# RWKV operands and triangular inverses in one program, row turns behind the pair products, and the samples' new states built in the layout of the output

## The chip, the cores and the metric

One core of a Trainium2 chip runs the whole step. The metric is the device time of one execution in microseconds. Of the kernel before, three timed runs gave a median of 1883.43 us (1877.42, 1883.43, 1886.05).

## The reference, cut to what matters

Two decoder layers are run for 256 prompt tokens and for 8 samples of 8 tokens each (320 token columns). The change lies in the RWKV-7 head group of the first layer (8 heads of 64):

```python
def rwkv7_scan(r, w, k, v, a, b, S0):
    def step(S, inp):                       # S is [value, key], per head
        rt, wt, kt, vt, at, bt = inp
        sa = jnp.einsum('bhvk,bhk->bhv', S, at)
        S = S * wt[:, :, None, :] + sa[..., None] * bt[:, :, None, :] + vt[..., None] * kt[:, :, None, :]
        return S, jnp.einsum('bhvk,bhk->bhv', S, rt)
    S, y = lax.scan(step, S0, xs)
    return y, S
```

Its final S is an output: `new_rwkv_prompt` (one state, 8 heads of 64 x 64) and `new_rwkv_sample` (8 states of that size). Before and after it stand the projections and the latent attention (MLA); behind it the output projection, a dense SwiGLU, the GLA layer and a mixture of 8 experts.

## The kernel before, in words

The step is a chain of parts. Between two parts stands `next_part()` (L154 to L159): all engines meet at a barrier, the semaphores are cleared, and they meet again. Inside a part every engine has its own list of instructions, written out by hand in the order in which it runs, and the engines wait for one another on semaphores. A `with nc.Block()` is such a set of lists; its end also holds every engine until all are there. So nothing of a later block starts before the last engine of the earlier one is through. No weights are loaded in the RWKV part: its only transfers are its own inputs and its outputs, issued on SP's queue.

The RWKV part has three blocks. Tokens are in three tiles (`TILES`: two of 128 prompt tokens, one of the 64 sample tokens), and "turning" means a transpose on TensorE.

1. The operands block (L1188 to L1394). VectorE and ScalarE build the scaled vectors b (`bF`), k (`kF`), and the pair `AR` of a and r, all with features on the partitions. TensorE turns v into rows by token (L1356) and the samples' old states into `S0T` (L1382). Last it turns b and k into rows, `rowB` and `rowK`, six turns of up to four 128 x 128 blocks (L1393) in banks 0 to 3; VectorE (L1280) and ScalarE (L1325) take them out of the banks by turns. `bonus` (L1275) is finished before them.
2. The inverses block (L1396 to L1487). The products b·a and b·r of each tile (`pairs`, L1419, 64 x 64 weights, 128 columns) are masked into `BM` (L1456), and `XT` and `X` are begun from it (L1466 to L1468). Then come five levels (L1427) in which TensorE and VectorE take turns; k's pair products and their masked form `KM` are woven into the first three.
3. The states block (L1490 to the next `next_part`). Chunk by chunk the prompt's state advances (`step`, L1560; `advance`, L1671 and L1673), the part of the output that comes from the state is added (`from_state`, L1567; `y_add`, L1677), and U of the samples gives their output (L1635, L1636). ScalarE begins the layer norm's terms after the third `from_state` (L1761, L1762). The samples' new states are made head by head: VectorE spreads U and v over eight blocks of columns, one for a sample (`spread`, L1683 and L1684, two buffers), TensorE multiplies (L1577, L1578, 64 x 64 weights and 512 columns), VectorE adds the old state and multiplies by the decay (`new_state`, L1689, L1690). Only when all four pairs of heads are done does TensorE turn the prompt's and the eight samples' states into the outputs' layout (L1654), ScalarE and VectorE copy them out by turns (L1767, L1741), and SP stores them one by one, 128 KB each (L241).

## Time and profile before

| | |
|---|---|
| median of three runs | 1883.43 us |
| profiled execution, its own time | 1890.77 us |
| its span, first to last instruction | 1888.9 us |
| mean granted TensorE clock | 0.962 |
| TensorE busy / weight loads / VectorE / ScalarE | 1790.3 / 1148.9 / 666.3 / 353.5 us |
| MLA part's last work to the part behind RWKV's first | 330.79 to 492.80 us |

How to read it: a time such as 376.84 is in us from the start of the span, "x80" is the number of records (a float32 matmul leaves two, a turn one), and "[0.93 <-PEq L1189]" says how long the engine had been idle before the line and what ended that. In the tables by stretch, PEclk is the granted clock: 1.00 is 2.4 GHz, 0.50 is 1.2 GHz. "PEld" is the weight load.

### The profile page before, as it was taken

How to read it: one execution, taken by the hardware profiler on the slowest of the kernel's cores; microseconds unless marked ns; L12 is line 12 of the kernel's file. 1: busy time of each engine (PE TensorE's matmuls, PEld its weight loads, DVE VectorE, ACT ScalarE, POOL GpSimd, SP SyncE). 2: the span in 40 equal slices, each digit the busy share in tenths (PEclk: the TensorE clock that was granted, in tenths of full speed). 3: DMA queues.
4: the chain of work that ended last, by engine and by line, in shares of the span. 5: the costliest groups of instructions: out<-in, count | busy, mean ns of one | idle time of the engine just before them, and what ended most of it. 6: DMA issues, size and time to landing. Idle time of an engine off the chain costs nothing.

```text
span 1888.9 us, 42360 instructions
## 1 busy us (share of the span) xinstructions
PE 1790.3 (95%) x19238; PEld 1148.9 (61%) x19238; DVE 666.3 (35%) x1243; ACT 353.5 (19%) x584; POOL 29.7 (2%) x37
## 2 busy tenths in 40 slices
PE   7989898689799999998999999999999999999997
PEld 6957564587599999996833535344353443535344
DVE  4534332774675554656642110121102111120121
ACT  3223231501243332444310000000000000000002
POOL 0010000000000000000000000000000000000000
PEclk9989998698799999999989999999999999999998
DMA  9130540200654444425499999999999999997994
GB/s 289 45 109 1 150 142 11 37 3 2 181 155 142 150 145 126 155 68 150 143 379 416 417 412 417 397 382 417 364 417 373 405 409 366 417 354 290 399 416 159
DMA packets 166440, 463.28 MB, mean 245 GB/s; under 512 B 27770, under 2 KB 110876, under 8 KB 135412
## 3 DMA queue, kind: packets, MB, share of 16 engines
q1 hardware_dynamic: 164910, 457.37, 65.2%
q8 instruction: 151, 2.47, 0.5%
q0 software_dynamic: 1152, 3.15, 0.4%
q14 instruction: 29, 0.24, 0.0%
q10 hardware_dynamic: 198, 0.05, 0.0%
HBM read 451.57 MB, written 8.95 MB: 244 GB/s over the span
## 4 chain that ended last, share of the span: by engine, by line
PE 52%; DVE 1%; ACT 0%; issue 0%; DVEq 0%; ACTq 0%
PE bank L2623 46%; PE bank L2591 1%; PE bank L310 1%; PE bank L312 1%; PE bank L311 1%; PE bank L2554 0%; PE bank L2475 0%; PE bank L2597 0%; PE bank L2561 0%; PE bank L2490 0%; PE bank L2509 0%; PE bank L2482 0%; ACT ring L2787 0%; DVE mixT L2805 0%; PE bank L2494 0%; PE bank L2686 0%
## 5 line engine op out<-in xcount | busy, mean ns | idle before, releaser
L2623 PE MATMUL bank<-ring,x 128*32 128x512 f32 (+1 forms) x6144 | 587.5, 540 | 0.0
L2623 PEld LDWEIGHTS bank<-ring,x 128*32 128x32 f32 x6144 | 195.0, 110 | 359.9 <-issue 357.2
L2623 PE MATMUL bank<-ring,hid 128*32 128x256 f32 x5376 | 291.5, 379 | 0.0
L2623 PEld LDWEIGHTS bank<-ring,hid 128*32 128x32 f32 x5376 | 174.7, 110 | 117.1 <-issue 3.1
L310 PE MATMUL bank<-x_hi,w_hi 128*128 128x320 f32 (+1 forms) x488 | 151.8, 311 | 0.0
L312 PE MATMUL bank<-x_hi,w_lo 128*128 128x320 f32 (+1 forms) x488 | 150.8, 309 | 0.0
L311 PE MATMUL bank<-x_lo,w_hi 128*128 128x320 f32 (+1 forms) x488 | 150.8, 309 | 0.0
L2129 DVE TENSOR_TENSOR w_lo<-ring,w_hi 128x2048 fp32r<-128x2048 f32 (+2 forms) x51 | 112.5, 2208 | 96.2 <-ACT w_hi L2053 95.9
L2987 DVE TENSOR_TENSOR hrow<-sil,bank 128x512 f32<-128x512 f32 (+1 forms) x48 | 26.9, 616 | 296.1 <-PE bank L2623 296.1
L2950 DVE TENSOR_TENSOR xT<-xT,bank 128x320 f32<-128x320 f32 x56 | 23.5, 483 | 277.4 <-PE bank L2591 277.4
L2053 ACT ACTIVATE w_hi<-ring 128x2048 fp32r<-128x2048 f32 (+2 forms) x51 | 94.1, 1846 | 128.9 <-PE bank L312 124.3
L2769 ACT ACTIVATE sil<-bank 128x512 f32<-128x512 f32 (+1 forms) x48 | 22.6, 544 | 478.9 <-PE bank L2623 478.9
L310 PEld LDWEIGHTS bank<-x_hi,w_hi 128*128 128x128 f32 (+1 forms) x488 | 90.9, 186 | 1.9 <-issue 1.0
L311 PEld LDWEIGHTS bank<-x_lo,w_hi 128*128 128x128 f32 (+1 forms) x488 | 90.9, 186 | 0.6 <-issue 0.2
L312 PEld LDWEIGHTS bank<-x_hi,w_lo 128*128 128x128 f32 (+1 forms) x488 | 90.9, 186 | 0.4
L2776 ACT ACTIVATE Y<-bank 128x256 f32<-128x256 f32 x24 | 7.5, 384 | 403.8 <-PE bank L2623 403.8
L310 PE MATMUL bank<-hid,w_hi 128*128 128x320 f32 x240 | 75.2, 313 | 4.1 <-DVE w_lo L2129 4.1
L311 PE MATMUL bank<-hid,w_hi 128*128 128x320 f32 x240 | 74.8, 312 | 0.0
L312 PE MATMUL bank<-hid,w_lo 128*128 128x320 f32 x240 | 74.8, 312 | 0.0
L2969 DVE COPY listed<-bank 32x2 f32<-32x2 f32 x108 | 16.5, 153 | 145.9 <-PE bank L2597 144.5
L310 PE MATMUL bank<-proj_x_hi,proj_w_hi 128*128 128x320 f32 (+1 forms) x160 | 51.2, 320 | 6.5 <-DVE proj_w_lo L587 6.5
L311 PE MATMUL bank<-proj_x_lo,proj_w_hi 128*128 128x320 f32 (+1 forms) x160 | 50.5, 316 | 0.0
(569 smaller groups left out, 2209.7 us busy)
## 6 DMA issues: line engine op xcount, KB each, us to landing
ring<-in_moe_w_gu SPq DMA_DIRECT2D x128, 1024.0 KB, 15.9
ring<-in_moe_w_down SPq DMA_DIRECT2D x112, 1024.0 KB, 13.1
ring<-in_moe_w_gu SPq DMA_DIRECT2D x128, 768.0 KB, 10.7
ring<-in_ffn_w_gu_even SPq DMA_DIRECT2D x44, 512.0 KB, 4.9
pages<-in_cache_mla SPq DMA_DIRECT2D x128, 144.0 KB, 2.4
ring<-in_w_in_odd SPq DMA_DIRECT2D x12, 1024.0 KB, 5.6
ring<-in_ffn_w_down_even SPq DMA_DIRECT2D x10, 1024.0 KB, 5.1
proj_ring<-in_w_in_even SPq DMA_DIRECT2D x9, 1024.0 KB, 8.0
```

The source lines that it names most:

```text
L310: t.matmul(out, w_hi, x_hi, start=start, stop=False)
L311: t.matmul(out, w_hi, x_lo, start=False, stop=False)
L312: return t.matmul(out, w_lo, x_hi, start=False, stop=stop)
L2053: s.activation(whi[:, i % NSP, 0:size(i)], ring[:, i % NS, 0:size(i)], ACT.Copy).then_inc(hi_ready, 1)
L2129: v.tensor_tensor(wlo[:, i % NSP, 0:size(i)], ring[:, i % NS, 0:size(i)], whi[:, i % NSP, 0:size(i)].bitcast(F32), ALU.subtract).then_inc( ...
L2591: mm = t.matmul(ps[banks[y]][:, 0:TOK], Y[part, s_, z * P:(z + 1) * P], selT[part, s_, :], start=(s_ == 0), stop=(s_ == SG - 1), tile_posi ...
L2623: mm = t.matmul(ps[banks[g3]][SL * y:SL * y + SL, 0:w], act[:, g3, k, :], m_ring[:, slot, at + y * w:at + (y + 1) * w], start=start, stop= ...
L2769: ins = s.activation(sil[:, s_, 0:quarter(g)], ps[s_][:, 0:quarter(g)], ACT.Silu)
L2776: s.activation(Y[:, s_, :], ps[bank][:, 0:256], ACT.Copy).then_inc(y_ready, 1)
L2950: last = v.tensor_tensor(xT[:, 2 * y + z, :], xT[:, 2 * y + z, :], ps[bank][:, 0:TOK], ALU.add)
L2969: last = v.tensor_copy(listed[SL * y:SL * y + SL, s_, :], ps[6][SL * s_:SL * s_ + SL, 0:2])
L2987: ins = v.tensor_tensor(hrow[:, 512 * s_:512 * s_ + n], sil[:, s_, 0:n], ps[3 + s_][:, 0:n], ALU.mult)
```

## The change

- The operands and inverses blocks become one block, with no meeting of the engines in between. The order of TensorE's list changes: the b pair products of the three tiles come first, as soon as `AR`, `bonus` and the `S0T` copies are done; the rows of b and k are turned behind them, in banks 6 and 7, and all go out of the banks on ScalarE. VectorE copies no rows.
- VectorE multiplies the samples' b and k by their decay at the end (`bks`, eight instructions of 128 x 64) ahead of `bonus`. The fifth turn puts the decayed b rows of the samples into partitions 0 to 63 and the k rows into 64 to 127 of `rowB[:, 2]`. Likewise the samples' v rows are made a second time in partitions 64 to 127 of `rowK[:, 2]` (four more matmuls and one ScalarE copy of 64 x 512), and U is later written into partitions 0 to 63 of it.
- VectorE begins tiles 0 and 1 of the inverse, takes the first level of tile 0, then begins tile 2.
- In the states block the rows of b and k, not those of U and v, are spread over the samples (`BKb`, 128 partitions, eight instructions in place of sixteen, four at the block's start and four between `rhs2` and the first state). `S0T` is multiplied by the decay there too, in place. TensorE then makes each new state already turned: for every sample and head one product of `S0T` with the identity and one of `UV2` (U over v, 128 partitions) with `BKb`, both with 64 weight columns and 64 columns moved, added in the bank: 128 products, in banks 0, 1, 4 and 6. There are no adds and decays behind them and no turns of the samples.
- Four copies take them out (VectorE pairs 0 and 2, ScalarE 1 and 3), and SP stores four times 256 KB, each for all samples and one pair of heads, then the prompt's state. `y_add(2)` now waits for the third `from_state`, as `y_add(3)` does.

The diff, cut to its core:

```diff
-                            for n in range(0, 6, 2):
-                                v.wait_ge(row_full, n + 1)
-                                r = TILES[n % 3][1]
-                                v.tensor_copy((rowB, rowK)[n // 3][0:r, n % 3, :], ps[n % 4][0:r, :]).then_inc(row_dve, 1)
+                            v.wait_ge(k_ready, 4)
+                            for n, src in enumerate((bF, kF)):
+                                for c in range(4):
+                                    last = v.tensor_tensor(bks[:, n, c, :].rearrange("p (b t) -> p b t", t=DS), src[:, c, SEQ:TOK].rearrange("p (b t) -> p b t", t=DS),
+                                                           wends[:, c, :].rearrange("p (b o) -> p b o", o=1).to_broadcast([P, NB, DS]), ALU.mult)
+                            last.then_inc(bks_ready, 1)
...
+                            v.wait_ge(st_full, NB)
+                            v.wait_ge(stored.sem, stored.n)
+                            begin(0)
+                            begin(1)
+                            for li in range(5):
+                                tiles = [i for i in range(3) if li < len(LEVELS[i])]
+                                for i in tiles:
+                                    r = TILES[i][1]
+                                    if li == 0 and i == 1:
+                                        begin(2)
...
-                            for n in range(1, 6, 2):
+                            for n in range(5):
                                 s.wait_ge(row_full, n + 1)
-                                r = TILES[n % 3][1]
-                                s.activation((rowB, rowK)[n // 3][0:r, n % 3, :], ps[n % 4][0:r, :], ACT.Copy).then_inc(row_act, 1)
+                                s.activation(ROWS[n], ps[6 + n % 2][:, :], ACT.Copy).then_inc(row_act, 1)
...
+                                    if i == 2:
+                                        t.matmul(ps[7][64:128, cols], vT[:, c, lo:lo + r], C("ident"), start=True, stop=True, tile_position=(0, 64))
...
+                            t.wait_ge(ar_ready, 1)
+                            t.wait_ge(bonus_ready, 1)
+                            t.wait_ge(st_free, NB)
                             for i in range(3):
-                                pairs(i, bF, (2 * i, 2 * i + 1)).then_inc(b_full, 1)
+                                pairs(i, bF, (2 * i, 2 * i + 1)).then_inc(pairs_full, 1)
+                            for n in range(5):
+                                t.wait_ge(*((k_ready, 4) if n < 4 else (bks_ready, 1)))
+                                if n >= 2:
+                                    t.wait_ge(row_act, n - 1)
+                                for c in range(4):
+                                    cols = slice(c * P, (c + 1) * P)
+                                    if n < 4:
+                                        src, lo = (bF, kF)[n // 2], TILES[n % 2][0]
+                                        mm = t.transpose(ps[6 + n % 2][:, cols], src[:, c, lo:lo + P], C("ident"))
+                                    else:
+                                        for q in range(2):
+                                            mm = t.matmul(ps[6][64 * q:64 * q + 64, cols], bks[:, q, c, :], C("ident"), start=True, stop=True, tile_position=(0, 64 * q))
+                                mm.then_inc(row_full, 1)
...
+                            def new_states(pr):
+                                for b in range(NB):
+                                    for h in (2 * pr, 2 * pr + 1):
+                                        hs, _, _ = head(h)
+                                        t.matmul(ps[N_BANK[pr]][hs, b * RD:(b + 1) * RD], S0T[:, b, pr, :], C("ident")[:, hs], start=True, stop=False, tile_position=(0, hs.start))
+                                        mm = t.matmul(ps[N_BANK[pr]][hs, b * RD:(b + 1) * RD], UV2[:, h * RD:(h + 1) * RD], BKb[:, h, b, :], start=False, stop=True,
+                                                      tile_position=(0, hs.start))
+                                mm.then_inc(n_full, 1)
...
-                            new_states((0, 1))
+                            t.wait_ge(blk_ready, 1)
+                            t.wait_ge(s0_ready, 1)
+                            new_states(0)
                             step(3)
+                            new_states(1)
                             from_state(3)
-                            new_states(range(2, RH))
+                            new_states(2)
+                            new_states(3)
...
+                            for pr in range(4):
+                                last = v.tensor_tensor(S0T[:, :, pr, :], S0T[:, :, pr, :], wends[:, pr, :].rearrange("p (b o) -> p b o", o=1).to_broadcast([P, NB, RD]), ALU.mult)
+                            last.then_inc(s0_ready, 1)
+                            for h in range(4, RH):
+                                last = spread(h)
+                            last.then_inc(blk_ready, 1)
...
+                            for pr in (1, 3):
+                                s.wait_ge(n_full, pr + 1)
+                                s.activation(news[:, pr, :, :].rearrange("p b k -> p (b k)"), ps[N_BANK[pr]][:, :], ACT.Copy).then_inc(n_act, 1)
+                            s.wait_ge(o_full, 1)
+                            s.activation(srow2, ps[5][0:RD, :], ACT.Copy).then_inc(o_act, 1)
...
+                            for pr in range(4):
+                                sp.wait_ge(n_act if pr % 2 else n_dve, pr // 2 + 1)
+                                store(sp, O["new_rwkv_sample"][0, :, 2 * pr:2 * pr + 2].rearrange("b h v k -> (h v) b k"), news[:, pr, :, :])
+                            sp.wait_ge(o_act, 1)
+                            store(sp, O["new_rwkv_prompt"][0, 0].rearrange("h v k -> v h k"), srow2.rearrange("v (h k) -> v h k", h=RH))
+                            sp.wait_ge(stored.sem, stored.n)
```

## Rows read from the trace of the kernel before

**Rows 1.** The page: span, then the chain of waits by engine.
```profile
span 1888.9 us, 42360 instructions
PE 52%; DVE 1%; ACT 0%; issue 0%; DVEq 0%; ACTq 0%
```
**Rows 2.** Timeline, end of the part: start us, us, engine, line, operation, [idle before].
```profile
480.73 5.92 PE L1654 MATMUL bank<-consts,S0T 128*64 128x128 f32 x32
...
481.59 0.64 SPq L241 DMA_DIRECT2D out_new_rwkv_prompt<-rwT  x1
482.54 6.08 SPq L241 DMA_DIRECT2D out_new_rwkv_sample<-rwT  x8
492.80 5.34 SPq L1895 DMA_DIRECT2D ring<-in_w_out_even  x4
```
**Rows 3.** Windows of one us: PE, PEld, DVE, ACT, POOL, PEclk, DMA share, GB/s.
```profile
482.00:483.00 1.00, 1.00 (x7) 0.84 (x5) 0.51 (x1) 0.32 (x1) 0.00 (x0) 0.50 0.08 13
...
484.00:485.00 1.00, 1.00 (x7) 0.82 (x6) 0.22 (x1) 0.59 (x1) 0.00 (x0) 0.50 1.02 157
...
490.00:491.00 1.00, 0.00 (x0) 0.00 (x0) 0.00 (x0) 0.00 (x0) 0.00 (x0) 0.50 0.65 95
```
**Rows 4.** Timeline, from the operands into the inverses.
```profile
337.33 0.28 DVE L1211 TENSOR_TENSOR shT<-shT,vecs 128x112 f32<-128x112 f32 x1
...
372.48 1.68 DVE L1275 TENSOR_TENSOR bonus<-bank,rwT 128x320 f32<-128x320 f32 x4
...
376.84 4.13 PE L1419 MATMUL bank<-hT,bF 64*64 64x128 f32 x80 [0.93 <-PEq L1189]
378.89 1.29 DVE L1456 TENSOR_TENSOR BM<-bank,consts 128x512 f32<-128x512 f32 x2 [2.68 <-PE bank L1419]
...
389.14 1.86 PE L1427 MATMUL bank<-X,BM 64*64 64x64 f32 x15 [1.80 <-DVE X L1468]
```
**Rows 5.** Timeline, TensorE and VectorE behind the v rows.
```profile
360.56 2.30 PE L1368 MATMUL bank<-consts,dif 128*128 128x128 f32 x12
362.80 1.68 DVE L1257 TENSOR_TENSOR t<-t,bank 128x320 f32<-128x320 f32 x4
```
**Rows 6.** Timeline of the states block, VectorE and ScalarE, then two of TensorE.
```profile
444.88 0.67 DVE L1703 TENSOR_TENSOR rhs<-rhs,bank 64x512 f32<-64x512 f32 x1
449.03 0.42 DVE L1705 TENSOR_TENSOR ST<-bank,wend 128x256 f32<-128x256 f32 x1 [3.48 <-PE bank L1553]
458.36 0.67 DVE L1683 TENSOR_TENSOR ub<-U,consts 64x512 f32<-64x512 f32 x1
458.96 0.68 DVE L1684 TENSOR_TENSOR vb<-rowV,consts 64x512 f32<-64x512 f32 x1
463.18 1.92 ACT L1761 ACTIVATE hT<-bonus,vecs 128x320 f32<-128x320 f32 x4 [6.09 <-PE bank L1567]
465.00 1.25 ACT L1762 ACTIVATE hT<-gT 128x1280 f32<-128x1280 f32 x1
...
L1623 PE MATMUL bank<-rhs,XT x16: 218/218/218, 450.5 to 451.4; 64*64 64x64 f32 x16
...
458.36 0.66 PE L1567 MATMUL bank<-hT,ST 64*64 64x64 f32 x16
```
**Rows 7.** Count, ns min/median/max, first and last start; last a line of the timeline.
```profile
L1636 PE MATMUL bank<-KM,rowV x16: 218/218/218, 457.1 to 457.9; 64*64 64x64 f32 x16
L1066 PE MATMUL bank<-mixT,uv x32: 222/222/270, 329.2 to 330.1; 128*64 128x64 f32 x32
396.61 1.09 PE L1427 MATMUL bank<-T,XT 64*64 64x64 f32 x16
```
**Rows 8.** Timeline, a weight load behind a change of the array's form.
```profile
442.26 1.72 PEld L1606 LDWEIGHTS bank<-AV,XT 64*64 64x64 f32 x32 [0.20 <-issue]
```
**Rows 9.** Windows: granted clock of two stretches (columns as in rows 3).
```profile
434.00:436.00 2.00, 2.00 (x28) 2.00 (x29) 0.00 (x0) 0.00 (x0) 0.00 (x0) 0.50 0.00 0
456.00:458.00 2.00, 2.00 (x77) 2.00 (x75) 1.07 (x3) 0.66 (x2) 0.00 (x0) 1.00 0.00 0
```

More of the change, by code:

```diff
@@ L1189, in model, with heads @@
+                    LEVELS = [[2, 4, 8, 16, 32], [2, 4, 8, 16, 32], [2, 4]]
+                    BLOCKS = [2, 2, 1]
+                    def heads(bank, r=P):
+                        return ps[bank][0:r, :].rearrange("p (h t) -> p h t", h=RH)
+                    ROWS = [rowB[:, 0, :], rowB[:, 1, :], rowK[:, 0, :], rowK[:, 1, :], rowB[:, 2, :]]
                     with nc.Block() as block:
@@ L1276, in _, with masked @@
                             last.then_inc(bonus_ready, 1)
[L1277 to L1280 removed]
                             v.wait_ge(bonus_ready, 1)
+                            def masked(dst, i, banks, ready):
+                                r = TILES[i][1]
+                                m = C("rw_T" if i < 2 else "sm_T", r).rearrange("p (o a t) -> p o a t", o=1, a=2).to_broadcast([r, 4, 2, RC])
+                                for par in range(2):
+                                    last = v.tensor_tensor(dst[0:r, i, :, :, :].rearrange("p (c e) a t -> p c e a t", e=2)[:, :, par, :, :],
+                                                           ps[banks[par]][0:r, :].rearrange("p (c a t) -> p c a t", c=4, a=2), m, ALU.mult)
+                                last.then_inc(ready, 1)
@@ L1490, in model @@
+                inv.close()
                 with ExitStack() as st:
@@ L1568, in from_state @@
                                 mm.then_inc(y_full, 1)
-                            def new_states(hs_):
-                                for h in hs_:
-                                    h0, pr = 64 * (h % 2), h // 2
-                                    t.wait_ge(blk_ready, h + 1)
-                                    if h % 2 == 0 and pr >= 2:
-                                        t.wait_ge(n_ready, pr - 1)
-                                    out = ps[pr % 2][h0:h0 + 64, :]
-                                    t.matmul(out, rowB[0:64, 2, h * RD:(h + 1) * RD], ub[:, h % 2, :, :].rearrange("p b v -> p (b v)"), start=True, stop=False)
-                                    mm = t.matmul(out, rowK[0:64, 2, h * RD:(h + 1) * RD], vb[:, h % 2, :, :].rearrange("p b v -> p (b v)"), start=False, stop=True)
-                                    mm.then_inc(n_full, 1)
+                            def new_states(pr):
[6 more added lines that the diff above has]
+                                mm.then_inc(n_full, 1)
                             for i in range(2):
```

205 lines of the change are left out of this document (72 added, 133 removed).

## The prediction
> **What bounds the kernel now.** I read four views in this order. First the page: the chain that ended last lies on TensorE in the last layer [rows 1], far behind the change. It says nothing of the RWKV part, for `next_part()` puts a barrier in front of and behind it, so a microsecond taken out there comes out of the total, if nothing behind depends on absolute time, and nothing does: the next weights are asked for only at 492.80, after the barrier [rows 2]. So the part has to be read by itself, from its timeline. In it the last thing is a tail: the reader sees 32 sample turns from 480.73 to 486.65 (plus four of the prompt ahead of them) and nine stores issued from 481.59 to 488.62 [rows 2]. The windows show when those stores end: the DMA engines are idle until nearly 483, then full at some 157 GB/s, and at 490.65 they stop (0.65 of the last us) [rows 3]. The first instruction behind the barrier comes 2.15 us later. So the part ends on its output bytes: 9 x 131 KB = 1.18 MB, at 150 to 157 GB/s 7.6 to 7.9 us, begun only when the last turn chain begins. The timeline of the border between the first two blocks shows a smaller thing: `bonus` is ready at 374.16, yet the first pair product starts at 376.84 [rows 4], because row turns, their copies and the block's end stand between.
>
> **Part by part.**
>
> *Samples' v rows a second time.* Four more float32 products of 128 moved columns, about 0.21 us each, so 0.85 us on TensorE, and one ScalarE copy. What stands behind them is the chain to the spread norms (360.56 to 362.86), taken by VectorE from 362.80 on without idle time before it [rows 5]. The first of the four norm banks needs three of the twelve turns, so it is full near 361.4, 1.4 us before VectorE comes. Shifted by 0.85 it is 0.5 us early, and the later ones come 0.58 us apart against 0.42 us per use, which is about level at the fourth. I take 0; without that cover it costs 0.9.
>
> *`bks`.* Eight VectorE instructions of 128 x 64. The nearest rows: 128 x 112 takes 0.28 us [rows 4]; 512 columns take 0.68 at a pace of 0.60 [rows 6]. That is 0.8 ns a column, so 64 columns last 0.24 and pace 0.17: 8 x 0.17 = 1.36. Bounds: 8 x 0.08 = 0.6 (no fixed cost) and 8 x 0.28 = 2.2. It delays `bonus`, on which the pairs now wait: 374.16 + 1.36 = 375.5.
>
> *One block for two.* Pairs start at 375.5 instead of 376.84: gain 1.3. VectorE masks 2.05 us later, as now (376.84 to 378.89) [rows 4]. The row turns leave VectorE (three copies) and come behind the 4.13 us of pairs, 379.6 on. They are paced by ScalarE, two banks, near 0.65 us each, so they end near 383. In that time VectorE runs begin(0) and begin(1) (3.4 us each, to 384.4), so TensorE's first level of tile 0 is late (383 instead of 381) but nobody is held: VectorE needs it at 384.4. Then comes one `T` (0.6) in front of begin(2), so that the level of tile 2, which opens the rest of the list, starts at 388.35 instead of 389.14 [rows 4]: of the 1.3 us 0.8 is left. Bounds: 0 (if `bks` is at its upper end) and 2 (below).
>
> *States block, front.* The first four spreads run at its start, where VectorE waits about 2 us for its first bank; the copy behind them is 0.4 late, needed only at 438.6. The other eight (four decays of `S0T`, four spreads, 128 x 512, pace 0.60) start when `rhs2` is done, 445.55, and last 4.9 us, to 450.4. The idle gap there is 3.48 us, up to 449.03 [rows 6]. So 1.4 us of them push the first state, and with it the emptying of bank 1 on which the own terms of chunks 2 and 3 wait. That wait was satisfied before TensorE came (U's product ends at 451.5 [rows 6]); now it ends near 451.9. I take +0.5 on TensorE's list, with 0 and 1.4 as bounds.
>
> *States block, products.* In place of 16 products of 512 columns there are 128 of 64 columns, in pairs on one half of the array, then the other. The output product of the samples has just this order: two added products on one half of the columns, then the other half; its 32 records (L1635 and L1636) start from 457.0 to 457.9, so 16 products in 0.95 us, 59 ns each. With 128 rows of weights as here, L1066 has 16 products in 0.95 too, 59 ns. Where all sit on the same tile, eight products of the level (396.61, 16 records) take 0.94 us, 117 ns each [rows 7]. I take 59: the order is that of the first row, and the shape is that of the second. A `new_states(pr)` is 32 x 0.059 = 1.9 us.
>
> A rule of the Trainium skill speaks against this part. First the row: where the weights' form goes from 128*64 to 64*64, the next load comes after 0.20 us of idle time [rows 8]. "TensorEngine Tiling (Array Packing)", Key Properties, says that changing the tiling mode, and not just the tile, drains TensorE. By that rule each swap between `new_states` (128*64) and `step` or `from_state` (64*64) costs, and there are five.
>
> Five such swaps at the 0.20 us of the row are 1.0 us; without them the part would end 0.7 earlier than below (the stores don't wait for all five).
>
> *The tail, put together.* `from_state(2)` ends its issue near 458.9 [rows 6]; the second advance no longer stands behind four spreads, so TensorE is not held there. With +0.5 and a little for `step(2)`: 459.6. Then new(0) to 461.65, step(3) 462.3, new(1) 464.35, `from_state(3)` 465.1, new(2) 467.1, new(3) 469.0, prompt's turns 469.5. ScalarE may start the norm's terms only behind `from_state(3)`, 465.2, and works 3.1 us on them (1.92 + 1.25) [rows 6]. So its first new-state copy is done at 468.9. SP's list is in order, so stores 1 to 4 leave from 469.0 on, and only store 0 (VectorE's, near 464.5) has landed by then. Issue to first bytes is 1.35 us (481.59 to some 482.9) [rows 2, 3]. Left are 3 x 262 + 131 KB = 0.92 MB, at 150 GB/s 6.1 us: 476.4. Plus 2.15 to the next part: 478.6. Now that is 492.8, so the tail gives 14.2.
>
> That assumes the rate of the present 256-byte pieces also for stores over 128 partitions. The pieces stay the same size, so I keep it; bounds 4 us (if more partitions feed it better) and 9 us (if SP or the engines need half as long again for 1024 pieces a store).
>
> *Sum.* 0.8 + 14.2 = 15.0 us. Own time of the profiled execution 1890.8 - 15.0 = 1875.8 (span 1888.9 to 1873.9). That execution is 7.3 above the median of the runs, which I carry along as an offset: 1883.4 - 15.0 = 1868.4.
>
> **The rivals.**
>
> *A. The products don't pair up.* Two products on the same tile in a row may each wait for the other's columns: 117 ns [rows 7]. For it: the 128-row row (L1066) changes halves after each product, this order only after two. Against it: L1635/L1636 change after two and reach 59. Price: a `new_states` is 3.75 us; the norm's terms start 3.7 later and new(3) ends at 476.5; the stores overlap better, store 3 leaves at 477.1, lands at 1.35 + 2.6 later = 481.1, next part 483.2. Gain 9.6 + 0.8 = 10.4: 1873.
>
> *B. Unpaired and at 1.2 GHz.* The granted clock fell to 0.50 in the samples' state products although TensorE was busy all the time; there 28 records stand in 2 us [rows 9]. At 0.50 a level on one tile took 1.86 us to the end of its 15th record (389.14), less 0.3 us for the last one's own length 0.21 for each product [rows 4]. 128 of them take 27 us, 19.6 more than forecast: new(3) ends near 488.6, store 3 leaves at 489.2, next part 495.3. Slower than before by 2.5 - 0.8 = 1.7, some 1885. It decides from about 0.19 us a product on. Against it: with as dense a list of 64-column products the clock stayed at 1.00 [rows 9]; the drop came with 16 columns.
>
> *C. The transfers bind harder.* The three late stores and the prompt's are the end of the part; at 9 us instead of 6.1 the gain is 12: 1871. For it: it is already what ends the part. Against it: same bytes, same pieces.
>
> *D. Gain by clock.* The row turns keep TensorE at work from 375.5 to 383. The present level of tile 2 and the work behind it run at half clock (0.21 us a product at 389.14 [rows 4] against 0.117 [rows 7]). If the clock stays up, about 1 us more is won: 1867.
>
> **How the numbers follow.** Forecast with D inside it 0.72, C 0.10, A 0.13, B 0.05. What a measurement of this kernel tells from no change is 0.5%, 9.4 us, so faster means below 1874.0. The forecast misses that only by the spread of the runs (1877 to 1886 before): a twentieth. C keeps it mostly, A lies on its edge (half), B is "same" or, with the spread, slower. Faster: 0.72 x 0.95 + 0.08 + 0.06 = 0.82, a little less for what no row shows: 0.80. Slower 0.03, same 0.17. Range: bounds of the terms are -1 to +3 around the sum of 15 for rows and `bks`, 2 to 3 for the stores, 3 for the spread of the medians; it reaches up to A: 1861 to 1875.
>
> **What would show it.** Pairs (L1419's successor) start near 375.5, with `bonus` ending at the same time; if they start later, `bks` or the norms' chain was dearer. Level of tile 2 near 388.3. The products of one pair of heads in 1.9 us at clock 1.00. The norm's terms on ScalarE start near 465, first new-state copy by it near 468, and the DMA engines are full from about 470 until 476. Next part's first load near 478.6. It is wrong if a `new_states` takes over 3 us, if the last store ends after 480, or if the front of the states block is over 1.5 us late.

## The result, and the profile after

Of the changed kernel 14 runs gave a median of 1869.36 us (1863.67 to 1881.84), beside 1886.08 (1876.17 to 1893.05, 14 runs) for the kernel before: a ratio of 0.9919, with an interval of [0.9899, 0.9939]. By this ratio that is 15.3 us less (11.5 to 19.0); the medians themselves lie 16.7 apart. 15.0 was forecast, and the median is 1.0 above the 1868.4. The changed kernel was measured again beside the last experiments: 1866.4 (6 runs), 0.9911 [0.9882, 0.994].

The profiled execution took 1863.67 us. Its page, span and chain, answers [rows 1]: the chain is what it was, and still says nothing of this part.

```profile
span 1861.8 us, 42751 instructions
PE 52%; DVE 1%; ACT 0%; issue 0%; DVEq 0%; ACTq 0%
```

This span is 27.1 us shorter than that of before, which is more than the change gave. The part itself runs from its first load (332.69 before, 324.66 after) to the next part's first load (492.80 before, 468.04 after): 160.11 against 143.38 us, 16.7 less. The other 10 us lie in code that is the same in both, 8.0 ahead of the part and 2.3 behind it; the last section comes back to that. **So all that follows is told by the part's own clock, from its first load on.** To set a time of after beside one of before, add 8.0.

SP's timeline at the end of the part, in answer to [rows 2] (of the last row only the start is read):

```profile
456.13 6.21 SPq L237 DMA_DIRECT2D out_new_rwkv_sample<-rwT  x4
462.38 1.18 SPq L237 DMA_DIRECT2D out_new_rwkv_prompt<-rwT  x1
468.04 2.34 SPq L1892 DMA_DIRECT2D ring<-in_w_out_even  x3
```

Windows of the last stores, columns as in [rows 3]. The engines are full again, as they were before, but now they move 215 to 218 GB/s instead of 157, and they stop near 465.9; the barrier's other side follows some 2.15 us later, as before:

```profile
462.00:463.00 1.00, 0.00 (x0) 0.00 (x0) 0.00 (x0) 0.03 (x1) 0.00 (x0) 1.00 1.07 218
463.00:464.00 1.00, 0.00 (x0) 0.00 (x0) 0.00 (x0) 0.00 (x0) 0.00 (x0) 1.00 1.05 215
...
465.00:466.00 1.00, 0.00 (x0) 0.00 (x0) 0.00 (x0) 0.00 (x0) 0.00 (x0) 0.50 0.95 161
```

The border, in answer to [rows 4]. The reader is to see three things: `bks` takes 0.54 us per four; TensorE has been idle for 3.62 us when the pairs start, and they last 5.25 us instead of 4.13; and VectorE waits 1.24 us before it can take `T` from the first level's products:

```profile
364.38 0.63 DVE L1292 TENSOR_TENSOR sample_bk<-bF,wends 128x64 f32<-128x64 f32 x4
364.92 0.63 DVE L1292 TENSOR_TENSOR sample_bk<-kF,wends 128x64 f32<-128x64 f32 x4
365.46 1.68 DVE L1297 TENSOR_TENSOR bonus<-bank,rwT 128x320 f32<-128x320 f32 x4
367.25 5.25 PE L1457 MATMUL bank<-hT,bF 64*64 64x128 f32 x80 [3.62 <-DVE bonus L1297]
372.42 1.09 PE L1481 MATMUL bank<-consts,bF 128*128 128x128 f32 x8
375.27 1.09 PE L1484 MATMUL bank<-consts,sample_bk 128*64 128x128 f32 x16 [0.29 <-ACT rowK L1388]
376.29 2.08 PE L1465 MATMUL bank<-X,BM 64*64 64x64 f32 x64
377.49 0.69 DVE L1330 TENSOR_TENSOR T<-bank,consts 128x512 f32<-128x512 f32 x1 [1.24 <-PE bank L1465]
381.59 1.17 PE L1465 MATMUL bank<-X,BM 64*64 64x64 f32 x15 [3.22 <-DVE X L1318]
```

The second profile of the changed kernel (changed_again below) shows the same code with the pairs in 4.25 us and a wait of only 0.23, though TensorE had been idle for longer, 4.50 us:

```profile
377.22 4.25 PE L1457 MATMUL bank<-hT,bF 64*64 64x128 f32 x80 [4.50 <-DVE bonus L1297]
381.40 1.09 PE L1481 MATMUL bank<-consts,bF 128*128 128x128 f32 x8
386.46 0.69 DVE L1330 TENSOR_TENSOR T<-bank,consts 128x512 f32<-128x512 f32 x1 [0.23 <-PE bank L1465]
```

The two differ in when the clock was low. From the part's first load on, the granted clock was 0.50 from 41 to 47 us in the first profile and from 44 to 46 us in the second; the pairs started at 42.6 and 43.8.

The samples' new states, in answer to [rows 6, 7]: 128 products, added two by two, from 451.5 to 460.6, a step and a `from_state` between them, and the norm's terms and the first copy on ScalarE:

```profile
453.29 0.34 PE L1587 MATMUL bank<-BKb,rowK 128*64 128x64 f32 x4
453.56 0.68 PE L1572 MATMUL bank<-ST,PT 64*64 64x64 f32 x16
454.17 0.34 PE L1586 MATMUL bank<-consts,S0T 128*64 128x64 f32 x4
456.96 1.92 ACT L1758 ACTIVATE hT<-bonus,vecs 128x320 f32<-128x320 f32 x4 [7.32 <-PE bank L1579]
459.94 0.57 ACT L1762 ACTIVATE rwT<-bank 128x512 f32<-128x512 f32 x1
```

Milestones of every run, in us from the part's first load. "Level" is the time at which `X` of tile 2 is ready, "inverse" the start of VectorE's last addition in the inverse, "norm" ScalarE's first norm term, "clock" the granted clock from 20 to 26 us, where the norms are spread:

| kernel | clock | `bonus` starts | level | inverse | norm | end of part |
|---|---|---|---|---|---|---|
| before | 0.50 | 39.79 | 56.39 | 91.56 | 130.49 | 160.11 |
| changed | 0.98 | 40.80 | 56.87 | 91.77 | 132.30 | 143.38 |
| changed_again | 0.50 | 42.03 | 57.09 | 93.44 | 133.96 | 145.04 |
| border_only | 0.50 | 40.34 | 56.31 | 91.20 | 130.18 | 160.12 |
| old_border | 0.52 | 41.82 | 58.85 | 94.19 | 134.71 | 145.79 |
| one_half_first | 0.98 | 40.67 | 56.78 | 91.67 | 135.48 | 148.20 |
| turns_early | 0.50 | 42.06 | 54.57 | 90.53 | 131.05 | 142.15 |
| kept_busy | 0.50 | 41.87 | 55.70 | 90.58 | 131.12 | 142.19 |
| stores_64_rows | 1.00 | 40.85 | 56.77 | 91.66 | 132.19 | 144.19 |
| stores_4_samples | 0.50 | 41.94 | 57.08 | 93.46 | 133.99 | 145.23 |
| decay_early | 0.98 | 40.68 | 56.83 | 91.72 | 131.92 | 142.99 |
| output_first | 0.50 | 41.96 | 57.08 | 93.45 | 130.36 | 143.66 |
| v_rows_late | 0.50 | 40.79 | 57.25 | 93.45 | 133.98 | 145.06 |
| all_four | 1.00 | 40.73 | 53.24 | 88.14 | 124.71 | 138.03 |

In its two profiled executions the changed kernel's part is 16.7 and 15.1 us shorter than before's. Only the second has before's clock in the norms' stretch. Of before there is one profile, so how far its own part scatters is not known.

### The profile page after: what moved, and what is told of

The parts are those of the page before. It is cut to its first block, busy times and chain, and to the rows that moved or that the text cites. A ratio compares the mean times of both kernels' runs of the same rounds, so it can differ in the third digit from the quotient of the medians.

```text
span 1861.8 us, 42751 instructions
## 1 busy us (share of the span) xinstructions
PE 1763.4 (95%) x19446; PEld 1139.0 (61%) x19446; DVE 656.0 (35%) x1234; ACT 353.9 (19%) x585; POOL 29.6 (2%) x37
## 4 chain that ended last, share of the span: by engine, by line
PE 52%; DVE 1%; ACT 0%; issue 0%; DVEq 0%; ACTq 0%
PE bank L2620 47%; PE bank L2588 1%; PE bank L310 1%; PE bank L312 1%; PE bank L311 1%; PE bank L2551 0%; PE bank L2472 0%; PE bank L2594 0%; PE bank L2487 0%; PE bank L2506 0%; PE bank L2479 0%; ACT ring L2784 0%; DVE mixT L2802 0%; PE bank L2491 0%; ACT ring L2783 0%; DVE mix_lo L2806 0%
## 6 DMA issues: line engine op xcount, KB each, us to landing
ring<-in_moe_w_gu SPq DMA_DIRECT2D x128, 1024.0 KB, 15.3
ring<-in_moe_w_down SPq DMA_DIRECT2D x112, 1024.0 KB, 13.4
```

## The experiments

**border_only.** The kernel before with the change's border alone (one block, pairs first, rows turned behind them and taken out by ScalarE), with its old states block and neither `bks` nor second v rows.

```diff
+                            t.wait_ge(ar_ready, 1)
+                            t.wait_ge(bonus_ready, 1)
+                            t.wait_ge(st_free, NB)
                             for i in range(3):
-                                pairs(i, bF, (2 * i, 2 * i + 1)).then_inc(b_full, 1)
+                                pairs(i, bF, (2 * i, 2 * i + 1)).then_inc(pairs_full, 1)
+                            t.wait_ge(k_ready, 4)
+                            for n in range(6):
...
+                                    mm = t.transpose(ps[6 + n % 2][0:r, c * P:(c + 1) * P], (bF, kF)[n // 3][:, c, lo:lo + r], C("ident"))
```

> The kernel before with the border alone changed: one block, b pair products first, the six turns behind them in banks 6 and 7 out by ScalarE, VectorE begins tiles 0 and 1, then a level, then tile 2. No bks, old states block. Read from the trace, in us from the first load of the part (332.69 before, 324.66 after). Theory 1 (the forecast): the border is worth 1.3 + 1.4 for the missing bks = 2.2 at the level of tile 2, which stood at 56.45 before, so near 54.3, and the part lasts 160.1 - 2.2 = 157.9. Theory 2 (from the trace of the changed kernel: TensorE comes cold to the pairs and is then held by the turns, so that VectorE waits for its first level): the level of tile 2 near 55.6, VectorE waits about 1.2 for the first level, the part lasts about 159.2.

Measured: its one time is 1897.19 us (1882.32 for before beside it), but its part starts 7.2 us later than before's, behind code that is unchanged; the part lasts 160.12, as before (160.11). From the start of `bonus` the inverse's end comes at 50.86 instead of 51.77, 0.9 earlier, but `bonus` itself starts 0.55 later, and the part's end does not move. Neither theory's length came (157.9 and 159.2). VectorE waits here too, as the second theory had it:

```profile
382.02 5.28 PE L1444 MATMUL bank<-hT,bF 64*64 64x128 f32 x80 [3.55 <-DVE bonus L1290]
392.16 0.69 DVE L1322 TENSOR_TENSOR T<-bank,consts 128x512 f32<-128x512 f32 x1 [1.14 <-PE bank L1452]
```

So the border carries next to nothing of the gain.

**old_border.** The changed states block behind the old border: two blocks, turns ahead of the pairs in banks 0 to 3, copies on both engines, tile 2 begun before the first level (`bks` and the second v rows stay).

```diff
+                            for n in range(5):
...
+                                        mm = t.transpose(ps[n % 4][:, cols], src[:, c, lo:lo + P], C("ident"))
...
+                    with nc.Block() as block:
+                        @block.tensor
...
-                            t.wait_ge(ar_ready, 1)
-                            t.wait_ge(bonus_ready, 1)
-                            t.wait_ge(st_free, NB)
                             for i in range(3):
                                 pairs(i, bF, (2 * i, 2 * i + 1)).then_inc(pairs_full, 1)
-                            for n in range(5):
```

> The changed kernel with the old border put back: the five turns ahead of the pairs, copied out by VectorE and ScalarE by turns, the block's end between them and the pairs, tile 2 begun before the first level. Everything else as changed. The changed kernel's part lasts 143.4, its level of tile 2 stands at 56.9. Theory 1 (forecast, the new border is worth 2.2 net of bks): this part lasts 145.6. Theory 2 (the new border gives back most of its gain): 144.3, level of tile 2 near 57.8. Either way nearly all of the 16.7 us gained stays, because it is in the states block.

Measured: 1874.12 us, part 145.79, 14.3 less than before. From `bonus` to the part's end it takes 103.97, the changed kernel 102.58 and 103.01: in this kernel the new border is worth 1.0 to 1.4 us by these three profiles, the states block all the rest. (The 145.79 lie near the first theory's 145.6, but `bonus` came 1.0 later here than in the profile that both theories start from.) How the rest divides among the products that come out already turned, the adds and decays that are gone, and the stores was not run apart; that account is read from the timeline.

**one_half_first.** The same 128 products, but the eight samples of one head before those of the other, so that 16 products in a row lie on one half of the columns (rival A made true).

```diff
-                                for b in range(NB):
-                                    for h in (2 * pr, 2 * pr + 1):
+                                for h in (2 * pr, 2 * pr + 1):
+                                    for b in range(NB):
```

> The changed kernel with the two loops of new_states swapped, so that all 16 products of one head come before those of the other: always the same half of the array. Same products, same number. If the halves work beside each other only when they alternate, a product takes 117 ns instead of 59 (the single-tile level of the trace before), the four sets take 7.5 us longer, the norm's terms start 3.7 us later, and the part lasts some 5 to 6 us longer, near 149 (the stores overlap more). If the order does not matter, 143.4 as it is.

Measured: 1876.25 us, part 148.20, 4.8 longer than the changed kernel's in the same clock. First and last starts of its products, and one window of a us with 24 records, where the changed kernel's windows from 458 and from 459 have 42 each:

```profile
L1586 PE MATMUL bank<-consts,S0T x128: 222/222/270, 459.8 to 475.2; 128*64 128x64 f32 x128
470.00:471.00 1.00, 1.00 (x24) 1.00 (x23) 0.00 (x0) 1.00 (x2) 0.00 (x0) 1.00 0.00 0
```

From the same view the changed kernel's go from 451.5 to 460.5, and a `new_states` takes 1.9 to 2.0 us there. With the loops swapped one product begins 117 ns behind the other, and a `new_states` takes 3.7 us. The order alone decides between 59 and 117 ns a product.

**turns_early.** Turns 0 and 1 before the pairs of tile 0, turns 2 to 4 before those of tiles 1 and 2, in banks 2 and 3; only tile 2's pairs wait for `bonus`. TensorE works while VectorE makes `hT` to `bonus`.

```diff
+                            turn(0)
+                            turn(1)
+                            t.wait_ge(ar_ready, 1)
+                            pairs(0, bF, (0, 1)).then_inc(pairs_full, 1)
+                            turn(2)
+                            turn(3)
+                            turn(4)
+                            t.wait_ge(row_act, 5)
+                            pairs(1, bF, (2, 3)).then_inc(pairs_full, 1)
+                            t.wait_ge(bonus_ready, 1)
+                            pairs(2, bF, (4, 5)).then_inc(pairs_full, 1)
```

> The changed kernel with the turns of b and k moved into TensorE's idle 3.6 us before the pairs: two turns, pairs of tile 0, three turns, pairs of tiles 1 and 2, the turns in banks 2 and 3. Theory 2 (the turns behind the pairs hold the first level, and TensorE comes cold to the pairs): VectorE begins tile 0 at once behind bonus, 2.2 us earlier than now, and does not wait 1.24 us for the first level: the level of tile 2 comes 3.4 us earlier, at 53.5 from the start of the part, and the part lasts 140.0 to 141.5. Theory 1 (what is left of the border is bound by bonus, and the turns are free where they are): no change, 143.4.

Measured: 1869.84 us. From `bonus` the level is reached at 12.51 instead of 16.07 (changed) or 15.06 (changed_again), and the part's end at 100.09 instead of 102.58 or 103.01. Because `bonus` came at 42.06 here, 1.26 later than in the profile that the expectation was taken from, the part as a whole (142.15) misses the 140.0 to 141.5 that were expected, and the level (54.57) the 53.5. VectorE no longer waits:

```profile
380.68 1.15 PE L1465 MATMUL bank<-X,BM 64*64 64x64 f32 x32 [0.29 <-DVE X L1318]
383.92 0.65 DVE L1330 TENSOR_TENSOR T<-bank,consts 128x512 f32<-128x512 f32 x1
```

Of the 3.6 us at the level, 1.1 are given back in the levels behind it, where its granted clock is 0.50 from 52 to 60 us (in the changed kernel's first profile it is 1.00 to 56 us, then 0.95 to 58).

**kept_busy.** The changed kernel with 32 turns of `bF` into an unused bank ahead of the pairs: work that nobody needs, put where TensorE is idle.

```diff
+                            t.wait_ge(st_free, NB)
+                            t.wait_ge(k_ready, 4)
+                            for n in range(32):
+                                t.transpose(ps[0][:, (n % 4) * P:(n % 4 + 1) * P], bF[:, n % 4, 0:P], C("ident"))
```

> The changed kernel with 32 extra turns of 128 x 128 (their result is not used) on TensorE between the last state copy and its wait for bonus, where it is idle for 3.6 us. Nothing else moves. In the changed kernel the granted clock is 0.50 for most of the pairs, which last 5.25 us, and VectorE then waits 1.24 us for its first level. If the cold clock is what makes the turns hold the first level: the pairs last about 3 to 4 us (they took 4.13 before the change at a clock that rose half way), the wait for the first level falls to near 0, the level of tile 2 comes 1.2 to 2 us earlier than now, counted from the start of bonus (16.1 now). If the queue of turns alone does it: the pairs get shorter but the wait stays near 1.

Measured: 1875.23 us, with a part of 142.19. The clock is up when the pairs come, they take 2.84 us instead of 5.25, and the wait for `T` is gone:

```profile
378.06 2.84 PE L1457 MATMUL bank<-hT,bF 64*64 64x128 f32 x80
386.11 0.65 DVE L1330 TENSOR_TENSOR T<-bank,consts 128x512 f32<-128x512 f32 x1
377.00:379.00 2.00, 1.86 (x44) 1.66 (x45) 0.96 (x3) 0.00 (x0) 0.00 (x0) 1.00 0.00 0
```

From `bonus` the level is reached at 13.83, 2.2 earlier than in the changed kernel's first profile and 1.2 earlier than in the second, whose clock in the norms is the same as here. The part's end comes at 100.32, 2.3 and 2.7 earlier, although nothing was taken away and 3.7 us of work were added.

The turns stand where they stood, and `T` is no longer waited for: so it is the length of the pairs that decides whether the turns hold the first level. The unedited border gives the same in five more profiles. Where the pairs last 5.10 to 5.33 us (stores_64_rows, one_half_first, decay_early) VectorE waits 1.10 to 1.31, where they last 4.30 and 4.32 (output_first, stores_4_samples) it waits 0.29 and 0.31. In all three kernels that put work into the idle stretch (this one, turns_early, all_four) the granted clock is 1.00 from 40 to 48 us of the part; in no other profile is it. That the idle stretch is what lowers it is argued from this. The idle time alone does not foretell the pairs, though: 4.50 us of it stood ahead of pairs that took 4.25, and 3.62 ahead of pairs that took 5.25.

**stores_64_rows.** Each sample store cut into its two heads: the same bytes and pieces, 64 partitions a store, 0 to 63 and 64 to 127 by turns.

```diff
-                                store(sp, O["new_rwkv_sample"][0, :, 2 * pr:2 * pr + 2].rearrange("b h v k -> (h v) b k"), news[:, pr, :, :])
+                                for q in range(2):
+                                    store(sp, O["new_rwkv_sample"][0, :, 2 * pr + q].rearrange("b v k -> v b k"), news[64 * q:64 * q + 64, pr, :, :])
```

> The changed kernel with each of the four sample stores cut into two by head: 64 partitions and 512 pieces of 256 bytes each, as the stores of the kernel before had. The DMA engines moved 157 GB/s before and 217 GB/s in the changed kernel. If the number of partitions of a store sets the rate: 157 GB/s again, the last bytes some 1.5 to 2 us later, the part 145 (counted with the changed kernel's 143.4). If the length of a store (1024 pieces or 512) sets it, the same figures, and the next run tells the two apart. If it is the order of the addresses in memory alone, 217 stays.

Measured: 1866.66 us; from the norm's terms to the end 12.00 instead of 11.08. The 157 GB/s that were expected did not come. With stores of the two halves in turn the windows show a rate between before's 157 and the 217:

```profile
468.00:469.00 1.00, 0.00 (x0) 0.00 (x0) 0.00 (x0) 0.00 (x0) 0.00 (x0) 1.00 1.04 192
469.00:470.00 1.00, 0.00 (x0) 0.00 (x0) 0.00 (x0) 0.00 (x0) 0.00 (x0) 0.84 1.06 194
```

**stores_4_samples.** Each store cut the other way, into four samples each: again eight stores of 512 pieces, as in stores_64_rows, but over 128 partitions.

```diff
+                                for q in range(2):
+                                    store(sp, O["new_rwkv_sample"][0, 4 * q:4 * q + 4, 2 * pr:2 * pr + 2].rearrange("b h v k -> (h v) b k"), news[:, pr, 4 * q:4 * q + 4, :])
```

> The changed kernel with each of the four sample stores cut into two by samples: 128 partitions and 512 pieces each. If the partitions set the rate, 217 GB/s stays and the part lasts 143.4; if the length of a store sets it, 157 GB/s and some 145.

Measured: 1872.84 us; from the norm's terms to the end 11.24, 0.2 more than with four stores. The rate stays:

```profile
473.00:474.00 1.00, 0.00 (x0) 0.00 (x0) 0.00 (x0) 0.00 (x0) 0.00 (x0) 1.00 1.05 215
474.00:475.00 1.00, 0.00 (x0) 0.00 (x0) 0.00 (x0) 0.00 (x0) 0.00 (x0) 1.00 1.05 215
```

So the number of stores costs 0.2 us, and a store over 64 partitions is slower than one over 128, at the same bytes, pieces and number of stores. What makes 184 to 198 of before's 157 stays open: the stores of before drew on partitions 0 to 63 alone, and they also went to memory in another order (one sample each, all heads); no run has only one of the two.

**decay_early.** The four decays of `S0T` moved ahead of `WU`'s second half, into an idle gap of VectorE, and the last four spreads ahead of it too.

```diff
+                            for h in range(4, RH):
+                                last = spread(h)
+                            last.then_inc(blk_ready, 1)
+                            v.wait_ge(sy_full, 1)
+                            for pr in range(4):
+                                last = v.tensor_tensor(S0T[:, :, pr, :], S0T[:, :, pr, :], wends[:, pr, :]...)
+                            last.then_inc(s0_ready, 1)
                             v.wait_ge(w_full, 2)
```

> The changed kernel with the eight VectorE instructions of the states block (four decays of S0T, four spreads) taken from behind rhs2 into the 12.5 us in which VectorE waits for its first WU copy, the decays behind the samples' state products. Theory: they push the emptying of bank 1 and so TensorE's own terms of chunks 2 and 3 by 0.34 to 0.5 us, and nothing else; so the third block gets 0.3 to 0.5 us shorter. Rival: the displacement costs nothing, because TensorE was not there yet; no change. A third: the decays wait for the state products, and the WU copy is late, which makes it longer.

Measured: 1861.96 us. From the inverse's end to the last `Q` on ScalarE it takes 32.22 us; the changed kernel 32.55, the kernel before 32.18. The displacement that the prediction put at 0.5 is 0.33 to 0.37.

**output_first.** Step 3 and the last `from_state` ahead of all new states, so that ScalarE can do the norm's terms beside them.

```diff
+                            step(3)
+                            from_state(3)
+                            t.wait_ge(q_dve, 2)
+                            t.wait_ge(q_act, 2)
+                            t.wait_ge(blk_ready, 1)
+                            t.wait_ge(s0_ready, 1)
                             new_states(0)
-                            step(3)
                             new_states(1)
-                            from_state(3)
                             new_states(2)
```

> The changed kernel with the last step and the last from_state ahead of all four sets of new-state products (three swaps of the array's form fewer). The norm's terms on ScalarE no longer stand behind two sets of products: they start 3.3 us earlier, near 129 from the start of the part (132.3 now), TensorE ends 0 to 0.5 us later or earlier, and the end is set by its last set of products, its copy and two stores. If the tail is bound by ScalarE's late start and the stores that queue behind it, the part gets 0.8 to 1.5 us shorter. If it is bound by TensorE's 128 products, it stays within 0.3.

Measured: 1869.08 us. The norm's terms come 3.6 us earlier (130.36 against changed_again's 133.96) and the end 1.4 (143.66 against 145.04). The copies now wait for TensorE, the other way round:

```profile
463.54 1.92 ACT L1758 ACTIVATE hT<-bonus,vecs 128x320 f32<-128x320 f32 x4 [3.71 <-PE bank L1579]
471.19 0.60 ACT L1762 ACTIVATE rwT<-bank 128x512 f32<-128x512 f32 x1 [3.14 <-PE bank L1587]
```

**v_rows_late.** The second v rows turned behind the turns of b and k instead of ahead of the spread norms.

```diff
-                                    if i == 2:
-                                        t.matmul(ps[7][64:128, cols], vT[:, c, lo:lo + r], C("ident"), start=True, stop=True, tile_position=(0, 64))
...
+                            t.wait_ge(row_act, 4)
+                            for c in range(4):
+                                mm = t.matmul(ps[7][64:128, c * P:(c + 1) * P], vT[:, c, SEQ:TOK], C("ident"), start=True, stop=True, tile_position=(0, 64))
```

> The changed kernel with the samples' second v rows (four products and one ScalarE copy) taken out of the operands and made behind the row turns. So far, in every run where the granted clock between 20 and 26 us of the part was 0.98 or more, VectorE took the spread norms without a wait (bonus starts at 40.7 to 40.9), and in every run where it was 0.50 it waited 0.4 to 0.6 and its four instructions lasted 2.20 instead of 1.67 us (bonus at 41.8 to 42.1). Theory: the four products at half clock are what breaks the cover: here bonus starts at 40.5 to 41.0 in either state of the clock. Rival: the clock alone does it: with 0.50 there, bonus still starts at 41.8 to 42.1. The moved work costs about 0.9 us of TensorE at the turns, so the first level waits up to 0.9 longer.

Measured: 1872.55 us. With the clock at 0.50, `bonus` starts at 40.79 (changed_again 42.03): its norms' line has no wait. First that line, then the one of changed_again; in the changed kernel's first profile, at clock 0.98, it lasts 1.67 without a wait (354.69):

```profile
363.22 1.67 DVE L1273 TENSOR_TENSOR t<-t,bank 128x320 f32<-128x320 f32 x4
```
```profile
364.14 2.20 DVE L1273 TENSOR_TENSOR t<-t,bank 128x320 f32<-128x320 f32 x4 [0.52 <-PE bank L1434]
```

The part is no shorter, 145.06 against 145.04: the products now stand ahead of the first level, where VectorE waits 1.63 us. From `bonus` to the level it takes 16.46 instead of 15.06, 1.4 more, where up to 0.9 was expected (the pairs are 0.5 longer here, 4.77 against 4.25). The cost had moved, not gone.

**all_four and changed_again.** turns_early, decay_early, output_first and v_rows_late together, and the changed kernel beside them, unedited.

> turns_early, decay_early, output_first and v_rows_late together. From the traces: 2.5 us by the turns in the idle gap (from bonus to the end of the part), 0.3 by the decays, 0.8 to 1.5 by output_first, 0 to 1.1 by the v rows: the part lasts 138 to 140 instead of 143.4 to 144.5, so 4 to 5 us under the changed kernel of the same call, and some 19 to 20 us (1.0%) under the kernel before. If the gains overlap (the stores end the part whatever comes before), the part lasts 141 or more.

> The changed kernel as it is, for comparison on the same chip. The part lasts 143.2 to 143.6 if the clock between 20 and 26 us of it is high, 144.4 to 145.2 if it is 0.50 (as in stores_4_samples, 145.2 with its own stores). Against the kernel before 15 to 17 us less.

Measured: all_four's part lasts 138.03 us against 145.04, 7.0 less: 1.3 at `bonus`, 2.55 from there to the level, 1.45 in the levels, 0.33 and 1.4 in the states block. In whole time it is not there: 1868.45 us (1865.4 to 1871.18, 6 runs), ratio 0.9921 [0.9894, 0.9948], against 1866.4 and 0.9911. Put together, the two intervals leave the difference between about -5.5 and +9.5 us. The two profiled executions are 2.1 us apart: 7.0 in the part, less 3.9 by which all_four's part begins later, less 1.0 behind it. Not all of the 7.0 is the edits'. The 1.45 in the levels go with the granted clock of the one execution (0.52 from 60 to 64 us in changed_again, 0.85 in the changed kernel's first profile, 1.00 in all_four); the 1.3 at `bonus` shrink to 0.07 beside the first profile, whose clock is up in the norms as all_four's is. Against that profile the part is 5.35 shorter, which lies at the edge of the interval. Whether something outside the part gives the gain back in every execution was not settled.

## Why the prediction was right, and where it was not

**What ends the part: right.** Norm's terms, copies, late stores, 2.2 us to the next load, in this order. Set in before's times, with the border's share (0.2 late at the inverse's end) taken out, the norm's terms start at 464.8 (forecast 465.2), the first copy by ScalarE at 467.8 (forecast 468.3).

**Products: right.** 59 ns at clock 1.00, 1.9 us a pair of heads. Rival A is a real mechanism (one_half_first pays 4.8 us for it) whose condition this order does not meet. Rival B did not occur (its 19.6 us should read 27 - 7.6 = 19.4). The five changes of form cost 0.12 to 0.15 us each: the last product pair of `new_states(0)` is followed by the step at 453.56, where its pace would give 453.41; forecast 0.20. "TensorEngine Tiling (Array Packing)", Key Properties, in the Trainium skill says that a change of mode drains TensorE, and this trace agrees in kind, with 0.12 to 0.15 us.

**Rate of the stores: mis-sized.** "That assumes the rate of the present 256-byte pieces also for stores over 128 partitions" was the failing term. The late 0.92 MB go at some 217 GB/s, 4.2 us instead of 6.1, and from the norm's start to the end it takes 11.08 us where the forecast has 13.4; rival C had the wrong sign. Bytes and pieces were the same as before, and stores_64_rows against stores_4_samples shows that the number of partitions a store draws on is a cause: it is worth the step from 184 to 198 up to 215. The rest, from 157, is open. The lower bound of 4 us had it, and it was not weighed any further. The Trainium skill has a rule for it that the prediction passed by: "SBUF — State Buffer", Door 1, says that a transfer's rate hangs on how many of 16 ports its partitions reach, and that partitions 0 to 63, like 64 to 127, reach half of them. The runs agree in direction; the rate rose by 1.4, not by 2.

**The border: wrong.** Forecast was a gain of 0.8 (the level's start 0.8 earlier). Measured are 0.5 later at the level and 0.2 later at the inverse's end in the first profile, 0.7 and 1.9 in the second. Up to the pairs the steps held in the first: `bks` costs 1.08 us (forecast 1.36), the pairs start 1.56 earlier (forecast 1.3). The failed step is the one behind: "so TensorE's first level of tile 0 is late (383 instead of 381) but nobody is held". The level came at 384.3 in before's times, and VectorE waited 1.24 us.

Three things went wrong in it. The pairs took 5.17 us to the first turn instead of 4.13, because the prediction took that time over from [rows 4], and here they met a granted clock of 0.50 for longer; kept_busy shows it by adding nothing but work ahead, turns_early by putting the needed work there. The five turns took 3.87 us instead of 3.4 (372.42 to 376.29). And the margin was not the 1.4 us between 383 and 384.4: the level's own products last 1.2 us (376.29 to 377.49) before `T` can be taken, so it was 0.2. The second profile shows what is left when the pairs take 4.18 as assumed: a wait of 0.23, and a level 15.1 us behind the start of `bonus`, where the forecast has 14.5 and the first profile 16.1.

The trace of before had a sign of the clock: its windows have it at 0.68 from 42 to 46 us of the part, where the pairs start, and that was not asked.

**v rows: right by the clock's grace.** "I take 0; without that cover it costs 0.9" holds where the clock is up in the stretch (0.98 or more: four runs, `bonus` at 40.7 to 40.9). At 0.50 to 0.52, in six runs, it comes at 41.8 to 42.1, and the cost is 1.1 (before's own 39.79 and the 1.08 of `bks` would give 40.87). v_rows_late, at 0.50 and without the rows, is back at 40.79.

**States block, front: right in kind**, 0.33 instead of 0.5.

**Rival D** did not come about as it was described, since the turns behind the pairs did not keep the clock up at tile 2's level in every execution: that line lasts 1.17 us in the first profile and 1.86 in changed_again, as before. Nor was it worth 1 us where the clock was up: from the level to the inverse's end it takes 34.90 in the first profile, 35.17 before, and 36.35 in changed_again.

So the sum was in part right by luck, by errors of opposite sign: in the first profile the border about 1.0 too good, the tail 2.7 too poor. In changed_again the part lasts 145.04, where the forecast has 145.1; there the late `bonus` and the slower levels make up for the tail as well.

## What to carry to other kernels

A duration read from the old trace holds only at the clock it had there: where work is moved away from in front of a dense stretch of TensorE, ask the windows what the clock is at the start of that stretch. Needed work put into the idle stretch paid twice here, by the turns gone from behind the pairs and by the pairs' own time. Count to the end of the products that an engine waits for, not to their start. Products with 64 columns, as here, should change halves of the array at least every second one. Give the last stores of a part all 128 partitions, even where bytes and pieces stay the same.

## What the runs showed of the hardware

- **Stores by partitions.** In 256-byte pieces: 157 GB/s from 64 partitions (0 to 63), 215 to 218 from 128, with 512 or 1024 pieces a store; 184 to 198 when stores of the two halves alternate (in another order of addresses than the 157).
- **The same code meets either clock.** In the norms' stretch it is 0.98 and more in four and 0.50 to 0.52 in six runs of the same instructions. That moves the part by 1.1 us there, and a low clock from 60 to 64 us (0.52 in changed_again, stores_4_samples and output_first) by 1.5 in the levels, so a single profile can't settle a term of that size; `bonus` was therefore used as the start wherever clocks differed.
- **Scatter ahead of the part.** The part starts anywhere from 324.66 to 339.90, behind code that is the same in all. Near 129 us the executions are still together to within 2.6 us (store of `new_mla_sample`), and at the page loads behind they are apart (187.51 after, 194.62 before, 198.43 in all_four). The granted clock goes with it: from 105 to 150 us it is 1.00 in the changed kernel's first profile, 0.81 in changed_again and 0.76 in all_four, whose parts begin at 324.66, 333.41 and 337.34. Scatter of this size can hide a gain of 5 us in a whole time. The windows, in this order:

```profile
105.00:150.00 45.00, 38.76 (x215) 26.54 (x215) 21.05 (x57) 14.80 (x41) 5.87 (x5) 1.00 0.36 109
```
```profile
105.00:150.00 45.00, 39.08 (x172) 25.58 (x170) 16.17 (x41) 11.65 (x31) 5.87 (x5) 0.81 0.39 113
```
```profile
105.00:150.00 45.00, 39.07 (x165) 25.76 (x164) 16.17 (x41) 11.24 (x30) 5.87 (x5) 0.76 0.36 105
```
